# Even block of a hybrid backbone: mLSTM values in another buffer, remainders and small loads in another order

## What is computed

```python
z = mod_1(h) @ ev_w_in          # q, k, v of 8 attention heads; xm, zv, zo, gates of 4 mLSTM heads
na = neighbourhood / context attention(q, k, v, rpb)
xc = silu(conv(xm)); ml = bidirectional mLSTM(xc Wq, xc Wk, v=zv, gates)
h  = LN(a*h + g_1 * concat(na, sigmoid(zo) * head_norm(ml)) @ ev_w_out)
```

## Time and profile before

| | |
|---|---|
| median of 3 runs | 2010.73 us (2009.46 to 2012.52) |
| the profiled execution: its own time | 2010.62 us |
| the profiled execution: its span | 2008.9 us |
| PE busy | 1876.0 us, 93% of the span |
| DVE busy | 1296.9 us, 65% |
| ACT busy | 675.5 us, 34% |
| POOL busy | 300.6 us, 15% |
| chain that ended last | PE 78%, DVE 13%, DMA 4%, ACT 4% |

### The profile page before, as it was taken

How to read it: one execution, slowest core, us unless ns; L and a number is a source line. 1 busy time by engine, 2 the same in 40 slices (tenths; PEclk the granted TensorE clock), 3 DMA queues, 4 the chain that set the end, 5 groups by cost and what they waited for, 6 DMA issues and landing times.

```text
span 2008.9 us, 24713 instructions
## 1 busy us (share of the span) xinstructions
PE 1876.0 (93%) x9400; PEld 1544.3 (77%) x9400; DVE 1296.9 (65%) x2254; ACT 675.5 (34%) x1139; POOL 300.6 (15%) x321
## 2 busy tenths in 40 slices
PE   5999999997996789899999989999999899989997
PEld 5888877896873455688887878888778867879997
DVE  7677776766984572877778357774677534465464
ACT  2322242344544431422224233222423232324453
POOL 0000001144000003400000231000045435130002
PEclk7999999998997899899999999999999999989999
DMA  9354544215431101354544233544134544214443
GB/s 359 124 199 185 187 163 164 93 55 126 151 138 68 43 1 42 147 203 174 199 159 175 87 153 124 197 182 151 79 118 191 220 188 176 84 43 168 171 167 123
DMA packets 43960, 290.13 MB, mean 144 GB/s; under 512 B 13916, under 2 KB 19676, under 8 KB 27232
## 3 DMA queue, kind: packets, MB, share of 16 engines
q1 hardware_dynamic: 35488, 271.13, 36.6%
q10 hardware_dynamic: 8384, 17.83, 2.3%
HBM read 272.16 MB, written 16.78 MB: 144 GB/s over the span
## 4 chain that ended last, share of the span: by engine, by line
PE 78%; DVE 13%; DMA 4%; ACT 4%; issue 1%; POOL 0%; SPq 0%; ACTq 0%; POOLq 0%; DVEq 0%
PE bank L654 13%; PE bank L659 13%; PE bank L656 13%; PE bank L711 6%; PE bank L720 5%; PE bank L717 5%; PE bank L1061 2%; PE bank L778 2%; DMA R<-in_ada_dram 2%; PE bank L768 1%; PE bank L1058 1%; DMA slot<-in_down_dram 1%; PE bank L825 1%; DVE g_lo L2077 1%; PE bank L869 1%
## 5 line engine op out<-in xcount | busy, mean ns | idle before, releaser
L1856 DVE CUSTOM_DVE_ANT_0 L<-slot 128x1024 f32<-128x1024 f32 x272 | 337.7, 1242 | 82.5 <-DMA slot<-in_ada_dram 75.3
L1245 ACT ACTIVATE w_hi<-slot 128x1024 fp32r<-128x1024 f32 x176 | 186.3, 1060 | 572.5 <-PE bank L659 561.2
L1904 DVE TENSOR_TENSOR w_lo<-slot,w_hi 128x1024 fp32r<-128x1024 f32 x176 | 217.0, 1235 | 210.2 <-ACT w_hi L1245 203.5
L654 PE MATMUL bank<-m_hi,w_hi 128*128 128x512 f32 (+1 forms) x1344 | 296.6, 363 | 3.2 <-ACT w_hi L1245 3.2
L659 PE MATMUL bank<-m_hi,w_lo 128*128 128x512 f32 (+1 forms) x1344 | 296.1, 362 | 0.0
L656 PE MATMUL bank<-m_lo,w_hi 128*128 128x512 f32 (+1 forms) x1344 | 296.1, 362 | 0.0
L654 PEld LDWEIGHTS bank<-m_hi,w_hi 128*128 128x128 f32 x1344 | 232.3, 189 | 43.1 <-ACT w_hi L1245 4.0
L659 PEld LDWEIGHTS bank<-m_hi,w_lo 128*128 128x128 f32 x1344 | 232.6, 189 | 39.3
L656 PEld LDWEIGHTS bank<-m_lo,w_hi 128*128 128x128 f32 x1344 | 232.6, 189 | 39.2
L2071 DVE TENSOR_TENSOR down_lo<-slot,down_hi 128x1408 fp32r<-128x1408 f32 x64 | 107.9, 1699 | 122.0 <-ACT down_hi L1295 121.8
L717 PE MATMUL bank<-g_lo,down_hi 128*128 128x512 f32 (+1 forms) x770 | 155.8, 350 | 0.1
(11 more groups left out here) (374 smaller groups left out, 2792.8 us busy)
## 6 DMA issues: line engine op xcount, KB each, us to landing
slot<-in_gateup_dram SPq DMA_DIRECT2D x44, 2048.0 KB, 7.9
slot<-in_ada_dram SPq DMA_DIRECT2D x34, 2048.0 KB, 7.9
slot<-in_down_dram SPq DMA_DIRECT2D x32, 1408.0 KB, 6.2
slot<-in_ev_in_dram SPq DMA_DIRECT2D x4, 2048.0 KB, 9.0
slot<-in_od_in_dram SPq DMA_DIRECT2D x4, 2048.0 KB, 9.8
R<-s_ops SPq DMA_DIRECT2D x16, 512.0 KB, 6.3
s_tables<-slot ACTq DMA_DIRECT2D x8, 768.0 KB, 3.3
R<-s_tables SPq DMA_DIRECT2D x8, 768.0 KB, 6.3
```

Of the source, the lines that this page charges most:

```text
L654: nc.tensor.matmul(bank[j][:, c0:T], w_hi[:, off, c, :], m_hi[:, c, c0:T], start=(c == 0), stop=False)
L1245: nc.scalar.activation(w_hi[:, off, :, :].rearrange("p a b -> p (a b)"), slots[b][:, (2 * (f % 2) + off) * D:(2 * (f % 2) + off + 1) * D], ...
L1856: ins = nc.vector.tensor_tensor_reduce(out=junk, in0=slots[k][:, t * D:(t + 1) * D], in1=csilu[s_], scale=1.0, scalar=0.0, op0=ALU.mult, o ...
L1904: nc.vector.tensor_tensor(w_lo[b][:, t, :, :].rearrange("p a b -> p (a b)"), slots[b][:, t * D:(t + 1) * D], w_hi[:, off, :, :].bitcast(F3 ...
```

## The change

Four things are edited. `ml_v` is placed in `R` from column 13312, over the rounded inputs, so ACT's copies of it no longer wait for the writes of operators, and that wait moves behind the attention's first exponentials. The order of DVE's remainders is moved: 6 comes ahead of the wait for the gate rows, 7 between the two sets of scans, and every entry of `REST_BEFORE` is one unit later in number, so that 20 is made before block 7. The raw operands of block b+2 are requested after a wait for `s5_blk_ready` of block b, in the unit ahead of the one that PE follows with block b, in place of after PE has turned block b. And `local_out(3)` comes behind the copies of `ml_v`, while POOL sets the ones beside `ml_v` once PE is done with slot 1, without waiting for the writes.

```diff
-REST_BEFORE = {0: (7,), 1: (8, 9), 2: (10, 11), 3: (12,), 4: (13, 14), 5: (15, 16), 6: (17,), 7: (18, 19)}
+REST_BEFORE = {0: (8,), 1: (9, 10), 2: (11, 12), 3: (13,), 4: (14, 15), 5: (16, 17), 6: (18,), 7: (19, 20)}
...
-        ml_v = slots[3][:, 1024:1024 + TT * HEADS * VCOLS].rearrange("p (t h n) -> p t h n", h=HEADS, n=VCOLS)
+        ml_v = R[:, 13312:13312 + TT * HEADS * VCOLS].rearrange("p (t h n) -> p t h n", h=HEADS, n=VCOLS)
...
                 act.wait_ge(sem("s5_blk_turned"), b + 1)
-                if b + 2 < len(BATCHES):
-                    raw_in(b + 2)
...
-                            if what == "ml_v":
-                                local_out(3)
-                                for b in range(2):
-                                    act.wait_ge(sem(f"s5_ops_written{b}"), 32 * (len(BATCHES) // 2))
-                                act.wait_ge(sem("s5_local_written"), 16 * (len(BATCHES) // 2))
...
                         s5_operators(b)
+                    if OPERATORS_BEHIND.get(u + 1, len(BATCHES)) + 2 < len(BATCHES):
+                        act.wait_ge(sem("s5_blk_ready"), OPERATORS_BEHIND[u + 1] + 1)
+                        raw_in(OPERATORS_BEHIND[u + 1] + 2)
+                local_out(3)
...
                 exps(0)
+                act.wait_ge(sem("s5_local_written"), 16 * (len(BATCHES) // 2))
+                for b in range(2):
+                    act.wait_ge(sem(f"s5_ops_written{b}"), 32 * (len(BATCHES) // 2))
...
                 part_rest(4)
                 part_rest(5)
+                part_rest(6)
                 dve.wait_ge(sem("even_soft"), 2)
...
                 scans(4, 2, ALU.add)
+                part_rest(7)
...
                 nc.vector.tensor_scalar(rows[:, 4:6, :], rows[:, 6:8, :], -1.0, None, ALU.mult)
-                part_rest(6)
...
-                part_rest(20)
                 s5_local_sum(3)
...
-                pool.wait_ge(sem("s5_local_written"), 16 * (len(BATCHES) // 2))
-                for b in range(2):
-                    pool.wait_ge(sem(f"s5_ops_written{b}"), 32 * (len(BATCHES) // 2))
+                pool.wait_ge(used[1], uses_before("even")[1] + 3)
                 nc.gpsimd.memset(ml_v[:, :, :, HDIM:VCOLS], 1.0).then_inc(sem("ml_ready"), 1)
+                pool.wait_ge(sem("s5_local_written"), 16 * (len(BATCHES) // 2))
```

More of the change, by code:

```diff
@@ L2613, in even @@
                     nc.gpsimd.memset(R[:, 12288:12800], 0.0).then_inc(sem("s5_zero"), 1)
+                pool.wait_ge(used[1], uses_before("even")[1] + 3)
+                nc.gpsimd.memset(ml_v[:, :, :, HDIM:VCOLS], 1.0).then_inc(sem("ml_ready"), 1)
                 pool.wait_ge(sem("s5_local_written"), 16 * (len(BATCHES) // 2))
-                for b in range(2):
-                    pool.wait_ge(sem(f"s5_ops_written{b}"), 32 * (len(BATCHES) // 2))
-                nc.gpsimd.memset(ml_v[:, :, :, HDIM:VCOLS], 1.0).then_inc(sem("ml_ready"), 1)
                 nc.gpsimd.memset(outside, 0.0).then_inc(sem("s5_zero"), 1)
```

## The result

| | before | changed |
|---|---|---|
| median | 2011.62 us (4 runs, 2009.46 to 2013.02) | 2030.97 us (4 runs, 2030.38 to 2032.7) |
| span of the profiled execution | 2008.9 us | 2031.0 us |
| PE busy | 1876.0 us | 1896.0 us |

The account below looks back on a forecast made before the run. PE, busy for 93% of the span, was taken to bound the kernel, so only its waits counted. The terms -1.0 + 21.8 - 3.4 - 10.0 = +7.4 on 2010.62 us gave 2018.0 us, range 2010 to 2024.5.

Parts of the forecast that it names:

- Block 0 and unit 6: The 11.67 us wait at unit 6 goes; PE waits 10.9 us ahead of block 0, tiles at 507.96: -1.0 us.
- The clock's price: At block 0, restarting at a low clock after the wait costs 1.8 us, bounds 0 and 2.6.
- The waits of part 2: Ahead of blocks 1 to 7, the later remainders' order makes PE wait 2.2 to 4.4 us each: +21.8 us in sum.
- Raw operands, -3.4: Earlier requests remove PE's 3.4 us wait at L798: -3.4 us, bounds -3.4 and 0.
- The end, -10.0: Ahead of L923, only the last of ACT's four `ml_v` copies is left of a 10.8 us stand: -10.0 us.
- What lies behind L923: Late `s_local` write (+1.3) and the attention's start at full clock, set together at 0, bounds -3 and +2.
- The rival of the cooled clock: New waits of 3.3, 4.4 and 4.4 us restart PE cold, each costing 1.8 more: 2023.4 us, chance 0.14.

Follow-up runs that it names:

- PE kept busy: Changed kernel plus extra 512-column matmuls, results unread, ahead of each wait for block tiles: 2019.75 us, ratio 1.0036.
- the order taken back: Changed kernel with remainders 6 and 7 as changed but the later ones in the order of before: 2002.24 us, ratio 0.9949.
- the last versions: Changed kernel with DVE reordered, blocks 0 and 1 made around the gate-row scans, 1993.97 us; the same with POOL's additions behind the clearings in groups, 1995.64 us.
- the version with the additions last: Changed kernel, later remainders as before, block 0's tiles made earlier, POOL's eight mask additions moved behind its three clearings: 1994.6 us, ratio 0.9912.

## Why the prediction was wrong

By its own steps:

- **Block 0 and unit 6: right in the waits.** No wait at L869 of unit 6, tiles at 508.00 for 507.96, a wait of 10.70 us for 10.9.
- **The clock's price: the step that failed.** "It ends at 507.96 + 2.58 + 1.8 = 512.3" took the 1.8 us from a restart with a large group of matmuls and gave them to a restart with small ones. Measured, it is 4.8 us at block 0 (the kernel with 46 matmuls in that wait). The bounds, "0 and 2.6, the whole work at half speed", ended at the end of the block; the low clock went on through the unit behind it. The same price was then left out at the other blocks. In all the term stands in the sum with 1.8 us, and the traces have it at 14.9, the changed kernel against the one with PE kept busy: 4.8 from block 0 to 1, 4.3 from 3 to 4, 1.0 from 4 to 5 and 4.8 from block 7 to L923.
- **The waits of part 2: right.** With the clock kept up each of the seven steps from tiles to tiles came within 0.4 us of its sum, although "every term has a row of its own" was too much said: the 1.6 for a rounding and a reading, the 1.5 for three copies and the 2.8 for block 4's had none. In the changed kernel the waits sum to 19.5 us for 21.8, and single ones are far off (6.22 and 2.08 for 4.4), since a PE at the low clock comes later itself. The kernel with PE kept busy came to +7.0 us, against a forecast of +7.4, or +5.6 without the clock's 1.8.
- **Raw operands, -3.4:** right in the change, where no wait for them is left (the 0.42 us at L798 are for ACT), but for a reason that the prediction did not have: PE came late. That is luck. Alone the earlier request saves 0.6 us of the wait, with the order taken back 0.8, and with PE kept busy 1.74 us of it are left. "8 us of PE's work before it is wanted" is not enough for a request that takes up to 11.7 us beside the loads.
- **The end, -10.0:** right, -9.2 alone and 0.88 us left at L923. What lies behind L923 costs 0.5 us, for 0.
- **The rival of the cooled clock** had the mechanism, and its 2023.4 us are still 7.6 short. It named the waits ahead of blocks 3, 5 and 7 and priced each at 1.8. Blocks 3 and 7 cooled PE, and so did block 4, which it did not name; block 5's wait was 2.08 us in place of 4.4, because PE was late itself, and did not.

The difference of 15 us between the changed kernel's trace and the forecast can be laid out by step, changed kernel against the forecast, each from the start of one block's tiles to the next: 0 to 1, 21.0 us for 17.8 with the 1.8; 1 to 2 and 2 to 3, as worked out (16.4 and 11.45 for 16.8 and 11.5); 3 to 4, 20.7 for 16.3; 4 to 5, 19.35 for 18.3; 5 to 6, 10.5 for 10.5; 6 to 7, 20.2 for 18.3; and from block 7 to L923, 14.0 for 9.0. That is 3.2 + 4.4 + 1.05 + 1.9 + 5.0, less 0.45, 15.1 us, and 7.4 + 15.1 = 22.5 of the 22.7 by which L923 is late. All but the 1.9 of step 6 to 7 lie where the clock was low. Those 1.9 are the landing of a local write: POOL's clearing came 4.3 us after the request (611.24 to 615.52), not the 2.4 taken from the earlier trace rows. In the kernel with PE kept busy it came after 2.4 us (603.80 to 606.23), and that step took the 18.3 worked out.

```profile
615.52 0.52 POOL L2613 MEMSET R<- 128x512 f32 x1 [31.20 <-DMA s_local<-R]
```

**What stays open** is which short wait cools PE. The old wait of 3.4 us at L798, on which I leaned, left the clock at 1.00; the 3.08 us ahead of block 3 did not, and neither did 3.11 and 5.68 at the same block in the last versions. Waits of 2.1 to 2.2 us left the clock at 1.00 ahead of blocks 1, 5 and 6 of the changed kernel, but it fell behind the 2.09 us of block 4, behind block 1's 2.10 in another kernel, and 1.7 us after the restart from block 7's 2.82 in a third (the version with the additions last). The Trainium skill, "TensorE: Matmul & The Clock Gate", the section on HAM oscillation, describes a kernel that restarts cold after each of its waits for data, of some 3 to 5 us. Here the waits of 10.70, 3.08 and 6.22 us agree with it, the wait of 3.35 us at L798 before does not, and the clock also fell behind waits of 2.09 and 2.10 us, shorter than those of its case.

## What to carry to other kernels

Price a wait of the tensor engine by what follows it: a restart into small matmuls cost 4.8 us more than the wait itself here, and one into large ones about 2. When a preparation step is moved ahead of the work that someone waits for, ask when its own input can be there. A remainder whose rounding must wait for a buffer to come free puts that whole round trip in front of the tiles, here at five of eight blocks. And a helper engine's idle time is a place for work only if no third engine holds it up there.

## What the runs showed of the hardware that I had not expected

- The full clock came back 4 to 5 us after a restart with large matmuls (4.0, and 4.8 with ten of them first; 5.3 with one large group and then a block's small ones), and 9 to 10 us after one with a block's small ones (10.2, 9.2 and 10.1 after waits of 10.70, 3.08 and 6.22 us).
- A request of 128 KB made 0.6 us ahead of a load of 2 MB on another queue landed after 11.7 us, with a median of 2.9 for its kind. In two other kernels one made 0.4 us ahead was waited for as well (2.32 us), and one made 0.8 us ahead was not.
- Beside POOL's additions DVE's small operations lost 3.5 to 4 us where all eight additions ran, and 3.1 and 2.1 us beside groups of three and of two, at whatever block they met. Among them were copies with one input. A remainder beside the additions took 1.73 us in place of 1.22:

```profile
480.28 1.73 DVE L2267 TENSOR_TENSOR w_lo<-slot,part_hi 128x1024 fp32r<-128x1024 f32 x1 [3.01 <-ACT part_hi L1489]
```
